# Attention rows of the second block: the softmax factors move from PE products of the output to GpSimd multiplications of the exponentials

## What is computed

```
def _masked_softmax(s, mask):
    ...
    e = jnp.exp(s - m)
    d = jnp.sum(e, axis=-1, keepdims=True)
    return e / jnp.where(d > 0.0, d, 1.0)
...
o = g[..., 0, :] * to_bthd(o_c) + g[..., 1, :] * to_bthd(o_s) + g[..., 2, :] * to_bthd(o_w)   # _nsa, 8 heads of 64
...
return jnp.einsum('bhqk,bkhd->bqhd', p.astype(v.dtype), v)      # _fox, 8 heads of 64, causal
...
p = jax.nn.softmax(s, axis=-1)                                  # _memory_xattn, 4 heads of 128, 256 keys
```

## Time and profile before

| what | value |
|---|---|
| time, median of 3 runs | 3434.85 us (3433.91 to 3436.3) |
| profiled execution: span from first to last instruction | 3435.4 us |
| mean granted clock of PE, of full speed | 0.981 |
| PE, DVE, ACT, POOL busy | 95%, 55%, 42%, 7% |
| second block, first layer | about 2060 to 2700 us |
| second block, second layer | about 2700 to 3436 us |

### The profile page before, as it was taken

How to read it: one execution, slowest core, us unless ns; L and a number is a source line. 1 busy time by engine, 2 the same in 40 slices (tenths; PEclk the granted TensorE clock), 3 DMA queues, 4 the chain that set the end, 5 groups by cost and what they waited for, 6 DMA issues and landing times.

```text
span 3435.4 us, 61486 instructions
## 1 busy us (share of the span) xinstructions
PE 3252.9 (95%) x26780; PEld 2575.1 (75%) x26780; DVE 1886.2 (55%) x2834; ACT 1437.4 (42%) x2518; POOL 253.8 (7%) x220
## 2 busy tenths in 40 slices
PE   8799999999998898899999998999999999999999
PEld 6577777788875687778788876767788767677787
DVE  6565657756465565557755654453444644534444
ACT  5544224434255443234423454454433445444432
POOL 0051330000000332500000000000000000000000
PEclk9899999999999999999999999999999999999999
DMA  4001103232231011123223231202122312111222
GB/s 156 22 21 45 39 27 124 99 98 92 97 113 50 8 33 51 34 72 120 92 95 95 81 119 63 85 26 68 53 92 77 107 46 89 44 59 63 76 71 95
DMA packets 75213, 249.16 MB, mean 73 GB/s; under 512 B 9281, under 2 KB 10945, under 8 KB 73921
## 3 DMA queue, kind: packets, MB, share of 16 engines
q1 hardware_dynamic: 74944, 245.22, 21.6%
HBM read 237.88 MB, written 6.29 MB: 71 GB/s over the span
## 4 chain that ended last, share of the span: by engine, by line
PE 80%; DVE 9%; ACT 6%; POOL 3%; issue 2%; DMA 0%; SPq 0%; POOLq 0%; ACTq 0%; DVEq 0%
PE psum L518 77%; PE psum L700 2%; POOL s_xb L2682 2%; DVE s_xb L1964 1%; ACT s_tmp L1260 1%; DVE s_tmp L1967 1%; ACT s_w L1260 1%; DVE s_nm L2046 1%; DVE s_ffy L1967 1%; DVE s_w L1964 1%; POOL s_tmp L2682 1%; ACT s_E L1260 1%; ACT L1260 1%; DVE s_tmp L1964 1%; ACT L1272 0%
## 5 line engine op out<-in xcount | busy, mean ns | idle before, releaser
L518 PE MATMUL psum<-s_h,s_w 128*128 128x512 f32 (+1 forms) x6864 | 1663.5, 399 | 28.8 <-DVE s_tmp L1967 18.0
L518 PEld LDWEIGHTS psum<-s_h,s_w 128*128 128x128 f32 (+1 forms) x6864 | 1286.4, 190 | 335.6 <-issue 46.5
L1964 DVE TENSOR_TENSOR s_w<-s_stage,s_w 128x1024 fp32r<-128x1024 f32 (+2 forms) x468 | 528.6, 1130 | 414.5 <-ACT s_w L1260 412.8
L1260 ACT ACTIVATE s_w<-s_stage 128x1024 fp32r<-128x1024 f32 (+2 forms) x468 | 451.3, 966 | 285.3 <-PE psum L518 263.5
L518 PE MATMUL psum<-s_ffa,s_w 128*128 128x512 f32 x1056 | 242.1, 390 | 4.6 <-DVE s_ffa L1964 4.6
L518 PEld LDWEIGHTS psum<-s_ffa,s_w 128*128 128x128 f32 x1056 | 197.8, 188 | 47.9 <-DVE s_ffa L1964 7.1
L518 PE MATMUL psum<-s_oR,s_w 128*128 128x512 f32 (+1 forms) x960 | 213.0, 373 | 0.0
L2046 DVE TENSOR_REDUCE s_nm<-psum 128x1 f32<-128x512 f32 (+3 forms) x288 | 138.1, 521 | 119.0 <-PE psum L518 118.5
L1260 ACT ACTIVATE s_E<-psum,s_nm 128x256 f32<-128x256 f32 (+3 forms) x224 | 114.5, 516 | 191.4 <-DVE s_nm L2046 191.4
L1967 DVE SCALAR_TENSOR_TENSOR s_ffy<-psum,s_pcol,s_ffy 128x511 f32<-128x511 f32 x176 | 131.7, 748 | 110.0 <-ACT s_ffy L1260 106.9
L1260 ACT ACTIVATE s_tmp<-psum 128x512 f32<-128x512 f32 (+2 forms) x154 | 87.7, 569 | 243.1 <-PE psum L518 237.9
(11 more groups left out here) (284 smaller groups left out, 3556.4 us busy)
## 6 DMA issues: line engine op xcount, KB each, us to landing
s_stage<-w SPq DMA_DIRECT2D x192, 512.0 KB, 3.2
s_stage<-wup SPq DMA_DIRECT2D x88, 512.0 KB, 3.2
s_stage<-wo SPq DMA_DIRECT2D x32, 512.0 KB, 3.2
s_stage<-wdn SPq DMA_DIRECT2D x32, 512.0 KB, 3.6
s_stage<-wdn SPq DMA_DIRECT2D x16, 384.0 KB, 3.1
spill<-s_x SPq DMA_DIRECT2D x2, 2048.0 KB, 8.9
s_stage<-woa SPq DMA_DIRECT2D x16, 256.0 KB, 2.7
s_x<-spill SPq DMA_DIRECT2D x2, 2048.0 KB, 7.9
```

The source lines that it names most:

```text
L518: return self.e.matmul(out, left, right, start=first, stop=last, skip_group_check=True)
L1260: return self.e.activation(out, src, func, **kw)
L1964: return self.e.tensor_tensor(out, a, b, op)
```

## The change

For the second block, 1/d and the gate are multiplied into the rows of exponentials before they are turned, and `factors` remains for the first block alone.

- `Attn` has a `lag`: 1 for `grid_attn` (first block, as before) and 2 for all others. With 2, `turn` stands two steps behind `score` and `pv` three; each attention loop has one more step. `s_E` has six buffers in place of four.
- ACT writes the sums of each unit into a ring `s_rows`; DVE inverts two numbers for each unit (`row_inverse`, into `s_inv`), right ahead of the maxima of the next unit.
- GpSimd multiplies each exponential tile in place by its column of `s_inv`, and in `_nsa` by the gate's column too (`shares`, one `tensor_scalar` for each head of a unit). `turn` waits for that.
- The spreading products, their PSUM bank, ACT's copy of it and DVE's multiplication go. DVE copies or adds the output straight from its bank.
- In `compressed`, DVE multiplies `s_cE` by `s_rc` before the turning, which now waits for this (`share`) where it waited for the exponential.

```
+    def __init__(self, q, k, v, klen, causal, row, E, PT, made, base, tile, dv=64, clear=(), lag=2):
+                [("vec_qk", (l, "q", 4), "out"), ("act_attn", l, "v")], 0, 0, clear=[("dma_spill", l)], lag=1)
...
-                self.w.wait_ge(*self.at("act_attn", tag, "e", U))
+                self.w.wait_ge(*self.at("pool_attn" if f.lag > 1 else "act_attn", tag, "e", U))
                 for c in range(n // 128):
                     last = self.e.transpose(ps[:, tile(c)], f.e(U)[:, tile(c)], m.cst[:, K_ID, :])
                 last.then_inc(*self.up("pe_turn", tag, U))
...
-            if p == f.np - 1:
+            if p == f.np - 1 and f.lag == 1:
                 ps = self.take((tag, "R", I))
-                self.w.wait_ge(*self.at("vec_attn", tag, ready, I))
+                self.w.wait_ge(*self.at("vec_attn", tag, "inv", I))
                 self.factors(ps, tag, f, I, m.ri[:, I % 2, :])
                 self.give((tag, "R", I), ("act_attn", tag, "R", I))
...
-        for u in range(len(units) + 3):
+        for u in range(len(units) + lag + 2):
             if u < len(units):
                 score(u)
             yield
-            if 2 <= u < len(units) + 2:
-                pv(u - 2)
-            if 1 <= u < len(units) + 1:
-                turn(u - 1)
-            if u >= 3 and units[u - 3][1] == f.np - 1:
-                I = f.tile + units[u - 3][0]
+            if lag + 1 <= u < len(units) + lag + 1:
+                pv(u - lag - 1)
+            if lag <= u < len(units) + lag:
+                turn(u - lag)
+            if u >= lag + 2 and units[u - lag - 2][1] == f.np - 1:
+                I = f.tile + units[u - lag - 2][0]
                 self.give((tag, "O", I), ("vec_attn", tag, "o", I))
             yield
...
-            self.w.wait_ge(*self.at("act_cmp", L, "e", i))
+            self.w.wait_ge(*self.at("vec_cmp", L, "share", i))
...
             last.then_inc(*self.up("pe_cmp", L, "O", i))
-            pr = self.take((L, "R", i))
-            self.w.wait_ge(*self.at("vec_cmp", L, "gated" if i else "valid", i))
-            self.factors(pr, L, f, i, m.rc[:, i % 2, 8:16])
-            self.give((L, "R", i), ("act_attn", L, "R", i))
-            self.give((L, "cO", i), ("vec_attn", L, "o", i))
+            self.give((L, "cO", i), ("vec_cmp", L, "added", i))
...
+                    total = m.rs[:, I % 2, 2 * p + e:2 * p + e + 1] if lag == 1 else m.rows[:, G % 8, e:e + 1]
                     self.f(f.e(U)[:, 0:n], self.bank((tag, "S", U))[:, 0:n], ACT.Exp, bias=m.nm[:, U % 8:U % 8 + 1],
-                           accum_out=m.rs[:, I % 2, 2 * p + e:2 * p + e + 1]).then_inc(*self.up("act_attn", tag, "e", U))
-            yield
-            if 2 <= u < len(f.units) + 2 and f.units[u - 2][1] == f.np - 1:
+                           accum_out=total).then_inc(*self.up("act_attn", tag, "e", U))
...
+        for u in range(len(f.units) + lag + 2):
+            if lag > 1 and 1 <= u < len(f.units) + 1:
+                self.row_inverse(tag, f.base + u - 1)
...
+    def row_inverse(self, tag, G):
+
+        self.w.wait_ge(*self.at("act_attn", tag, "e", 2 * G + 1))
+        if G >= 8:
+            self.w.wait_ge(*self.at("pool_attn", tag, "e", 2 * (G - 8) + 1))
+        self.e.reciprocal(self.m.inv[:, G % 8, :], self.m.rows[:, G % 8, :]).then_inc(*self.up("vec_attn", tag, "inv", G))
...
             def out(i):
                 I = f.tile + i
-                acc = m.otok[:, :, tile(i)]
+                acc, o = m.otok[:, :, tile(i)], v4(self.bank((L, "O", I)))
+                self.w.wait_ge(*self.at("pe_pv", L, f.base + 4 * i + 3))
                 if b == 0:
-                    self.scaled(L, I, acc)
+                    self.e.tensor_copy(acc, o).then_inc(*self.up("vec_attn", L, "o", I))
                     return
-                t = self.take((L, "nsa", I))
-                self.scaled(L, I, t)
-                self.w.wait_ge(*self.at("vec_attn", L, "o", I))
                 self.w.wait_ge(*self.at("vec_cmp", L, "added", i))
-                self.tt(acc, acc, v4(t), ALU.add).then_inc(*self.up("vec_attn", L, "sum", I))
-                self.give((L, "nsa", I), ("vec_attn", L, "sum", I))
-            return self.attention(L, f, out, ready)
+                self.tt(acc, acc, o, ALU.add).then_inc(*self.up("vec_attn", L, "o", I))
...
-                self.scaled(L, f.tile + i, m.otok[:, :, tile(i)])
+                self.w.wait_ge(*self.at("pe_pv", L, f.base + f.np * i + f.np - 1))
+                self.e.tensor_copy(m.otok[:, :, tile(i)], v4(self.bank((L, "O", f.tile + i)))).then_inc(*self.up("vec_attn", L, "o", f.tile + i))
...
-            yield
-            yield
-            self.w.wait_ge(*self.at("act_attn", L, "R", i))
-            t, acc = self.take((L, "cmp", i)), m.otok[:, :, tile(i)]
-            self.tt(t, self.bank((L, "cO", i)), self.tmp((L, "R", i)), ALU.mult).then_inc(*self.up("vec_attn", L, "o", i))
-            self.w.wait_ge(*self.at("vec_attn", L, "o", i))
+                self.w.wait_ge(*self.at("vec_cmp", L, "valid", 0))
+            self.tt(v3(E), v3(E), B(mx[:, 8:16, None], 2, 32), ALU.mult).then_inc(*self.up("vec_cmp", L, "share", i))
+            yield
+            yield
+            acc, o = m.otok[:, :, tile(i)], v4(self.bank((L, "cO", i)))
+            self.w.wait_ge(*self.at("pe_cmp", L, "O", i))
             self.w.wait_ge(*self.at("vec_attn", L, "o", 4 + i))
-            self.tt(acc, acc, v4(t), ALU.add).then_inc(*self.up("vec_cmp", L, "added", i))
-            self.give((L, "cmp", i), ("vec_cmp", L, "added", i))
+            self.tt(acc, acc, o, ALU.add).then_inc(*self.up("vec_cmp", L, "added", i))
...
+        for l in range(2):
+            for b in range(2):
+                self.shares(("B", l), nsa_attn(m, l, b), lambda i, h: m.g24[:, i, 12 * (h % 2) + 3 * (h // 2) + 1 + b:12 * (h % 2) + 3 * (h // 2) + 2 + b])
+            self.shares(("B", l), fox_attn(m, l))
+            self.shares(("B", l), mem_attn(m, l))
+
+    def shares(self, tag, f, gate=None):
+
+        m = self.m
+        for u, (i, p) in enumerate(f.units):
+            G, n = f.base + u, f.klen(i)
+            for e in range(2):
+                U = 2 * G + e
+                E, inv = f.e(U)[:, 0:n], m.inv[:, G % 8, e:e + 1]
+                self.w.wait_ge(*self.at("act_attn", tag, "e", U))
+                self.w.wait_ge(*self.at("vec_attn", tag, "inv", G))
+                if gate is None:
+                    self.e.tensor_scalar(E, E, inv, None, ALU.mult).then_inc(*self.up("pool_attn", tag, "e", U))
+                else:
+                    self.e.tensor_scalar(E, E, inv, gate(i, 2 * p + e), ALU.mult, ALU.mult).then_inc(*self.up("pool_attn", tag, "e", U))
```

75 lines of the change are left out of this document (31 added, 44 removed).

## The result

The changed kernel takes 3371.6 us (median of 4 runs, 3369.4 to 3376.1), the kernel before, run beside it, 3435.6; the ratio is 0.9813, with a 95% interval of 0.9801 to 0.9824. That is 64 us faster, where 53.6 us were forecast. The profiled execution took 3376.1 us with a span of 3374.1, 61.3 us less than before; it is the slowest of the four, which is why the spans differ by less than the medians.

The account below looks back on a forecast made before the run. PE was taken as the bound, busy 3252.9 of 3435.4 us. The terms -44.1 - 21.2 + 1 + 4.7 + 4 + 2 = -53.6 us gave a forecast of 3381 us, range 3365 to 3408.

Parts of the forecast that it names:

- What goes, on PE: Second block: PE's instructions with `s_ri` and `s_rc`, 46.9 us, less 2.8 us beside other work; gain 44.1 us.
- 0.07 us of each block lies beside other work: Spreading products on PE: each block ends 0.07 us after its successor starts; 40 blocks, 2.8 us off the gain.
- The waits for `s_ri`: PE's waits for the inverse sums, 8.9 and 1.7 us a layer, go wholly in both layers: 21.2 us.
- GpSimd: Its 224 multiplications, 1.1 us for 512 columns, are covered by PE's work of two units: price 0, upper end 12 us.
- between 0.7 and 1.5 us: Sign of being right: GpSimd's rows of 512 columns take this long.
- The wait before the maxima: DVE inverts the previous unit's sums before a unit's maxima, delaying a few short units: 1 us, ends 0 and 5.
- Tails: One more step of 0.78 us in the `_nsa`, `fox_attn` and `mem_attn` loops of each layer: 4.7 us.
- The compressed part: Turning stands behind sum, inversion, gate and multiplication; 1 us for each of two tiles a layer: 4 us, ends 0 and 8.
- The lock: GpSimd and DVE's weight splits block each other's way into SBUF: 2 us; as rival 24 us, 3403 us, chance 0.11.
- 14 to 18 us shorter: Sign of being right: the 64 us stretch without projections, in `_nsa` part b = 1, shrinks by this much.
- The renamed wait: Rival: PE waits for `s_PT` or the exponentials' bank instead of `s_ri`; 21.2 us come back, 3402 us, chance 0.15.
- GpSimd as the bound: Rival: GpSimd slows unfilled units of `_nsa` and `mem_attn`; deciding from 3.1 us per 512 columns, 3457 at 3.5; chance 0.08.

Follow-up runs that it names:

- e1: Changed kernel with the spreading products back on PE as mere work, operand always ready and result unused; 3405.84 us.
- e9: The kernel before with only the lag of 2 in the second block, spreading products, ACT's copies and DVE's multiplications kept; 3414.92 us.
- e3: Changed kernel without GpSimd's multiplications in the second block, so the output lacks division by the sums and gates; 3374.69 us.
- e4: Changed kernel with each of GpSimd's multiplications done twice, the first time by ones; 3393.93 us.
- e2: Changed kernel with a lag of 1 in place of 2 in the second block, GpSimd's multiplications kept; 3428.67 us.
- e7: Changed kernel with DVE's inversion of a unit's sums behind the next unit's maxima, not ahead of them; 3376.18 us.
- e6: Changed kernel with the compressed part as before: spreading products, ACT's copy and DVE's output multiplication back, turning waits for exponentials alone; 3383.07 us.
- e12: Changed kernel with plain multiplications given constant 1.0, projections spread beside `mem_attn` and delayed beside `fox_attn`, and ACT's `s_mv` copies half a step later; 3374.81 us.

## Why the prediction was right, and where not

The sum was -53.6 us of span; measured are -61.3 (-64.6 in the second block alone). The mechanism was right: products and waits both went, and GpSimd cost nothing. Several terms were not, and they partly made up for each other. By its terms:

- **What goes, on PE (-44.1).** PE's busy time fell by 45.6 us, but it is made of other parts: 33.6 us are the products (e1) and 12.0 are the same work done in less time, 10 at most by the clock. That 44.1 and 45.6 are so near is luck. The step that failed is "0.07 us of each block lies beside other work": I read it where the block came behind a wait; where it did not wait, the block starts before the output products end as well, and in e1 0.25 us of a block are covered. That is 7.0 us of the 10.5 too much. The other 3.5 are the other half of the step, counting blocks that ran at the lower clock in full: the same products keep PE busy for 43.4 us in e1 and for 46.9 before.
- **The waits for `s_ri` (-21.2).** They went, with the products (e1) and without (e9). But in e9 the rest fell by only 8.0 us (11.7 in the second block): 9.8 us came back as waits for `s_PT` (4.4 more on ACT, 3.0 on DVE) and `s_tmp` (2.4 more). With the factors' copies gone too the rest fell by 18.7 (e1). The step that failed is "ACT's copies of the factor bank, and DVE's multiplications by it, lie beside PE's work: nothing"; from e9 to e1 9 to 11 us went, and they are the most likely cause, if the names of the waits are right.
- **GpSimd (0).** Shown twice: e3 at zero, e4 where the slack ended. The cover named, PE's work of two units, is the right one: e2 takes half of it away and loses 57 us. I put one price on two forms; 0.77 and 1.61 us lie on either side of 1.1, and "between 0.7 and 1.5 us" holds for the gated form alone. That the prediction is wrong "if a multiplication of 512 columns takes over 1.7 us" was a poor bound: two of them took 1.97 us, each behind a weight split, and the time stayed; doubled to 3.2 (plain) and 1.5 us (gated), the kernel is still over 40 us faster than before.
- **The wait before the maxima (+1)**: PE waits 2.0 us for `s_inv`; by e7 it cannot be had cheaper by order.
- **Tails (+4.7)**: waits for `s_PT` rose by 3.0 us.
- **The compressed part (+4)**: 1.5 us for `s_cE`. The 4.7 us for `s_cPT` are no cost of it (e6); by the rows of e12 they come from a weight split.
- **The lock (+2, ends 0 and 24)**: 0. In the changed kernel two of 194 weight splits run while GpSimd multiplies, and 11 in a layer were assumed; GpSimd starts when DVE turns to the maxima, which read PSUM. DVE's splits, first in the changed kernel, then without GpSimd (ns min/median/max):

```profile
L1961 DVE TENSOR_TENSOR s_w<-s_stage,s_w x195: 424/1224/1228, 2059.6 to 3355.8; 128x1024 fp32r<-128x1024 f32 x146, 128x512 fp32r<-128x512 f32 x48, 128x256 fp32r<-128x256 f32 x1
```

```profile
L1961 DVE TENSOR_TENSOR s_w<-s_stage,s_w x194: 424/1224/1227, 2064.7 to 3354.8; 128x1024 fp32r<-128x1024 f32 x145, 128x512 fp32r<-128x512 f32 x48, 128x256 fp32r<-128x256 f32 x1
```

In e4, where 34 splits meet it, the loss can be seen on either side. A split that begins 0.14 us into a multiplication takes 1.63 us in place of 1.22, and a multiplication that begins 0.07 us into a split takes 2.59 us where the first line, ahead of its split, has 1.57:

```profile
2398.33 1.57 POOL L2704 TENSOR_SCALAR s_E<-s_E,s_inv 128x512 f32<-128x512 f32 x1
...
2398.47 1.63 DVE L1961 TENSOR_TENSOR s_w<-s_stage,s_w 128x1024 fp32r<-128x1024 f32 x1 [1.87 <-ACT s_w L1255]
...
2407.95 1.23 DVE L1961 TENSOR_TENSOR s_w<-s_stage,s_w 128x1024 fp32r<-128x1024 f32 x1 [1.56 <-ACT s_w L1255]
...
2408.02 2.59 POOL L2704 TENSOR_SCALAR s_E<-s_E,s_inv 128x512 f32<-128x512 f32 x1
```

The Trainium skill, page "SBUF — State Buffer", section "SBUF: two separate sides", says that whichever of the two starts first blocks the other for its whole instruction. Behind a split that comes nearly true: GpSimd lost 1.02 us to a split of 1.23. Behind a multiplication it does not: DVE lost 0.41 us to one of 1.57, and nothing in the changed kernel, where two splits begin 0.85 us into one. No run shows either on PE.

The forecast "14 to 18 us shorter" for the unfilled stretch compares ill: from its last projection to the next it was 63.6 us (2224.44 to 2288.04) and is 50.6 (2216.28 to 2266.83), 13 us less, and it now holds one more unit's scores.

**The rivals.** The renamed wait was true of one wait (e6) and of half of `s_ri`'s in e9; priced at all 21 us it was too dear. GpSimd as the bound did not come; e4 shows how it begins, in `mem_attn` and by its plain form.

Why 7.7 us more than forecast? PE's busy time gives 1.5 of them: 10.5 us too much for the products, less the 12.0 us of faster work, of which the range had only "some 5 us more" at its low end. The rest of the span gives 6.2: it was forecast to fall by 9.5 (21.2 less 11.7 of costs) and fell by 15.7. PE's waits in the second block went from 58.9 to 39.2 us, 19.7 less; the costs of order (`s_PT` 3.0, `s_inv` 2.0, `s_cE` 1.5) were 6.5 in place of 11.7, the lock's included, and `s_tmp` and `s_E`, less the `s_cPT` that took their place, gave 4.5 us that I had not counted. Some 3 us of the difference between 19.7 and 15.7 are the first block, which this change does not touch: the second block's marks came that much later in the profiled execution of the changed kernel (PE's first sums of `memory` at 2067.43 us against 2064.12).

The ends of the range do not all follow from their terms: 44.1 + 21.2 less 4.7 is 60.6, which gives 3374 and, with 5 us more, 3369 at the low end, not 3370 and 3365; and the upper ends of the two smaller costs give 3389, not 3395. The measured time lies inside either way.
